# Recurrence of 64-token chunks on one core: the triangular inverse's products of odd chunks placed on the crossed corners of the TensorE array

## The reference

```
def step(s, inp):
    r_t, w_t, k_t, v_t, kk_t, b_t = inp
    sa = jnp.einsum('bhij,bhj->bhi', s, kk_t)
    s = s * w_t[:, :, None, :] - sa[..., None] * b_t[:, :, None, :] + v_t[..., None] * k_t[:, :, None, :]
    return s, jnp.einsum('bhij,bhj->bhi', s, r_t)
```

## Time and profile before

| | us |
|---|---|
| median of 3 runs | 3148.85 (3147.89 to 3151.09) |
| the profiled execution's own time | 3144.85 |
| its span, first to last instruction | 3143.1 |
| recurrence, twelve passes (2066 to 2577) | 511.0 |
| PE busy in them | 437.73 |
| DVE busy in them | 337.21 |
| ACT busy in them | 245.44 |
| POOL busy in them | 237.93 |

### The profile page before, as it was taken

How to read it: one execution, slowest core, us unless ns; L and a number is a source line. 1 busy time by engine, 2 the same in 40 slices (tenths; PEclk the granted TensorE clock), 3 DMA queues, 4 the chain that set the end, 5 groups by cost and what they waited for, 6 DMA issues and landing times. The chain is left out here.

```text
span 3143.1 us, 59081 instructions
## 1 busy us (share of the span) xinstructions
PE 2825.9 (90%) x25000; PEld 2232.2 (71%) x25000; DVE 1862.5 (59%) x2779; ACT 1153.1 (37%) x2127; POOL 1023.7 (33%) x582
## 2 busy tenths in 40 slices
PE   7999898999989998999999799978888887699987
PEld 5765576877867655777878587857777775479975
DVE  6888656885059786478840466466666654354062
ACT  4234434333242334343321422244454533242252
POOL 1422142444424221334443222244444430132202
PEclk9999899999999999999999899989999997899988
DMA  6321123433323211244332423210000003033111
GB/s 214 94 77 51 42 87 96 147 114 90 98 80 91 74 41 55 74 136 144 117 88 81 127 78 104 81 49 23 4 24 23 24 8 137 31 111 91 54 38 54
DMA packets 349911, 247.85 MB, mean 79 GB/s; under 512 B 10811, under 2 KB 322385, under 8 KB 349137
## 3 DMA queue, kind: packets, MB, share of 16 engines
q1 hardware_dynamic: 342384, 228.05, 24.0%
q10 hardware_dynamic: 7264, 16.03, 1.6%
HBM read 221.59 MB, written 16.52 MB: 76 GB/s over the span
## 5 line engine op out<-in xcount | busy, mean ns | idle before, releaser
L540 POOL TENSOR_TENSOR weights_lo<-weights_raw,weights_hi 128x1024 fp32r<-128x1024 f32 (+2 forms) x230 | 582.0, 2531 | 1111.3 <-ACT weights_hi L509 1111.3
L1181 PE MATMUL psum<-moving_hi,weights_hi 128*128 128x512 f32 x1472 | 601.7, 409 | 40.5 <-PEq L178 13.7
L1181 PE MATMUL psum<-moving_lo,weights_hi 128*128 128x512 f32 x1472 | 581.7, 395 | 0.0
L1181 PE MATMUL psum<-moving_hi,weights_lo 128*128 128x512 f32 x1472 | 581.2, 395 | 0.0
L1181 PEld LDWEIGHTS psum<-moving_hi,weights_hi 128*128 128x128 f32 x1472 | 281.0, 191 | 160.8 <-issue 67.8
L509 ACT ACTIVATE weights_hi<-weights_raw 128x1024 fp32r<-128x1024 f32 (+1 forms) x240 | 248.3, 1036 | 249.3 <-PE psum L1181 244.5
L1181 PEld LDWEIGHTS psum<-moving_hi,weights_lo 128*128 128x128 f32 x1472 | 281.0, 191 | 60.8
L1181 PEld LDWEIGHTS psum<-moving_lo,weights_hi 128*128 128x128 f32 x1472 | 282.2, 192 | 56.3 <-issue 3.8
L2585 POOL TENSOR_TENSOR second_off<-second_mats,second_masks 128x256 f32<-128x256 f32 x180 | 140.7, 786 | 157.4 <-PE psum L2061 156.7
L2641 PE MATMUL psum<-hn_hi,even_hi 128*128 128x256 f32 x480 | 166.4, 347 | 8.6 <-DVE hn_lo L1998 7.7
L2641 PE MATMUL psum<-hn_lo,even_hi 128*128 128x256 f32 x480 | 164.1, 342 | 0.0
(11 more groups left out here) (468 smaller groups left out, 6137.7 us busy)
## 6 DMA issues: line engine op xcount, KB each, us to landing
weights_raw<-in_w_up SPq DMA_DIRECT2D x88, 512.0 KB, 3.7
weights_raw<-in_w_in SPq DMA_DIRECT2D x80, 512.0 KB, 3.7
ada<-in_ada_w SPq DMA_DIRECT2D x9, 2048.0 KB, 9.4
odd_raw<-in_od_w_in SPq DMA_DIRECT2D x16, 1024.0 KB, 5.5
even_raw<-in_ev_w_in SPq DMA_DIRECT2D x30, 512.0 KB, 4.0
weights_raw<-in_w_down SPq DMA_DIRECT2D x32, 448.0 KB, 3.7
weights_raw<-in_w_o SPq DMA_DIRECT2D x16, 512.0 KB, 4.0
weights_raw<-in_w_down SPq DMA_DIRECT2D x16, 512.0 KB, 3.9
```

Of the source, the lines that this page charges most:

```text
L540: ops.tensor_tensor(self.ring.lo[i % n][:, a:b], self.ring.raw[:, t % self.ring.landing, a:b], self.ring.hi[i % n][:, a:b].bitcast(F32), A ...
L1181: return nc.tensor.matmul(to, (hi, lo)[which][:, at:at + P], moving(k)[part], start=start and k == 0 and i == 0, stop=stop and k == n_k - ...
```

## The change

Chunks at odd places of a group (c = 1 and 3) keep their W<sup>T</sup> on the other head's half of the partitions (`turn_odd`, one transposition of 64 partitions for each half). Their Y is computed crossed, so it lies on the other half as well, and their increment is crossed back. Even chunks use the first bank of a pair and odd ones the second: Y lies in banks 0 and 1, the increment in banks 2 and 3, in each round. So Y(n) now waits for the copy of Y(n-1), and the increment of n-1 for the addition of n-2. At a group's beginning the whole transposition stays and `turn_odd` follows behind its own semaphore; after a level, one transposition of the two even chunks (`straight`) and the two of `turn_odd` take the place of the whole one. In the steps, p of an odd chunk stays crossed, since its W<sup>T</sup> is: its beginning becomes straight, its end and the u product crossed. The copy of Y and the addition go over the two banks in one instruction each, as before.

```diff
...
         return halves_matmul(self.nc, self.p, self.buf.ntrk[:, slot_of(self.i, self.order[k]), 0:CH], self.v(k),
-                             start=True, stop=k == 0, crossed=True)
+                             start=True, stop=k == 0, crossed=not self.turned(k))
+
+    def turned(self, k):
+
+        return (self.order[k] - self.starts[k // 4]) % 2 == 1
...
                 pe.wait_ge(self.state_ready, k)
-                halves_matmul(nc, self.p, b.ar[:, self.i % 3, n, 0:CH], b.st[:, k % 2, :], start=False, stop=True).then_inc(self.p_ready, 1)
+                halves_matmul(nc, self.p, b.ar[:, self.i % 3, n, 0:CH], b.st[:, k % 2, :], start=False, stop=True,
+                              crossed=self.turned(k)).then_inc(self.p_ready, 1)
                 self.begin_y(k - 1)
...
             pe.wait_ge(self.p_taken, k + 1)
-            halves_matmul(nc, self.u, b.wb[:, slot, 0:CH], self.p_sb).then_inc(self.u_ready, 1)
+            halves_matmul(nc, self.u, b.wb[:, slot, 0:CH], self.p_sb, crossed=self.turned(k)).then_inc(self.u_ready, 1)
             if k + 1 < NCH and (k % 4 or not g):
...
             over = lambda name: mask(name).unsqueeze(1).to_broadcast([P, 4, mask(name).shape[1]])
-            bank = lambda b, n: psum[:, b * 512:b * 512 + 4 * n].rearrange("p (c n) -> p c n", n=n)
...
                 .rearrange("p b (c n) -> p b c n", n=width)
-            bank_y, bank_w = lambda n: bank(n % 2, CH), lambda n: bank(2 + n % 2, CH)
+            bank_y, bank_w = (pair_of_banks(n, CH)[:, :, 0:2, :] for n in range(2))
+            straight = lambda x, g, to: x[:, slots(g).start:slots(g).start + 4:2, to]
+            turned = lambda x, g, to, hf: x[64 * hf:64 * hf + 64, slots(g).start + 1:slots(g).start + 4:2, to]
+            by_bank = lambda x: x.rearrange("p (c b) n -> p b c n", b=2)
+            T, W = slice(0, CH), slice(CH, 2 * CH)
             names = "unit_ready taken_act taken_dve wt_scaled wt_begun w_begun masked y_ready y_taken w_ready w_added wt_turned "
...
                             if level == 0:
-                                pe.wait_ge(w_begun, g + 1)
+                                pe.wait_ge(w_begun, 2 * g + 2)
                             else:
                                 pe.wait_ge(w_added, n - 2)
-                            if n >= 2:
-                                pe.wait_ge(y_taken, n - 1)
+                            if n:
+                                pe.wait_ge(y_taken, n)
                             for c in range(4):
-                                last = halves_matmul(nc, bank_y(n)[:, c, :], off[:, n % 2, c, :], buf.wb[:, slots(g).start + c, CH:])
+                                last = halves_matmul(nc, bank_y[:, c % 2, c // 2, :], off[:, n % 2, c, :], buf.wb[:, slots(g).start + c, CH:],
+                                                     crossed=c % 2 == 1)
                             last.then_inc(y_ready, 1)
...
                             pe.wait_ge(y_taken, n)
-                            if n > 2:
-                                pe.wait_ge(w_added, n - 2)
+                            if n > 1:
+                                pe.wait_ge(w_added, n - 1)
                             if level:
...
                                 wt, y_ = buf.wb[:, s0 + c, 0:CH], y[:, own(g).start + c, :]
-                                last = halves_matmul(nc, bank_w(n)[:, c, :], *((wt, y_) if level < last_level else (y_, wt)))
+                                last = halves_matmul(nc, bank_w[:, c % 2, c // 2, :], *((wt, y_) if level < last_level else (y_, wt)),
+                                                     crossed=level < last_level and c % 2 == 1)
                             last.then_inc(w_ready, 1)
...
                             act.wait_ge(y_ready, n + 1)
-                            S.activation(y[:, own(g), :], bank_y(n), ACT.Identity).then_inc(y_taken, 1)
+                            S.activation(by_bank(y[:, own(g), :]), bank_y, ACT.Identity).then_inc(y_taken, 1)
                         steps(len(units) + 2 * n)
...
+                    def turn_odd(g):
+                        for hf in range(2):
+                            last = V.transpose(turned(buf.wb, g, T, hf), turned(buf.wb, g, W, 1 - hf))
+                        return last
+
                     def begin_w(g):
                         dve.wait_ge(wt_begun, g + 1)
-                        V.transpose(buf.wb[:, slots(g), CH:], buf.wb[:, slots(g), 0:CH]).then_inc(w_begun, 1)
+                        V.transpose(buf.wb[:, slots(g), W], buf.wb[:, slots(g), T]).then_inc(w_begun, 1)
+                        dve.wait_ge(w_begun, 2 * g + 1)
+                        turn_odd(g).then_inc(w_begun, 1)
...
                                 dve.wait_ge(w_added, n - 1)
-                                V.transpose(buf.wb[:, slots(g), 0:CH], buf.wb[:, slots(g), CH:]).then_inc(wt_turned, 1)
+                                V.transpose(straight(buf.wb, g, T), straight(buf.wb, g, W))
+                                turn_odd(g).then_inc(wt_turned, 1)
                         if n:
...
                             w_ = buf.wb[:, slots(g), CH:] if level < last_level else buf.wb[:, slots(g), 0:CH]
-                            V.tensor_tensor(w_, w_, bank_w(n), ALU.add).then_inc(w_added, 1)
+                            V.tensor_tensor(by_bank(w_), by_bank(w_), bank_w, ALU.add).then_inc(w_added, 1)
                         steps(len(units) + 2 * n + 1)
...
```

## The result

The changed kernel takes 3200.4 us (3196.4 to 3204.1) against 3148.4 of before: 1.0166 times its time, interval 1.0154 to 1.0178, 52 us slower. The forecast was 3146 with a range up to 3168. The rest of the program is unchanged; the difference lies in the recurrence and its bare steps.

What follows compares the result with a forecast made beforehand. Compute and its hand-overs, not DMA, bound the recurrence. Passes -4.8, -2, +1, -2.5, corners +2.2 and clock +3 sum to -3.1 us, taking the 3148.85 median to 3146; range 3124 to 3168, the forecast's own 3140 to 3153.

Steps and rivals of the forecast that it cites:

- Takes away: TensorE's products in the rounds: 27 of 30 per pass become half crossed, each 0.21 us shorter, 68 us in all.
- Adds: VectorE's transpositions: 0.66 us a turn, 0.31 more, 45 us; groups' beginnings 0.91 instead of 0.35, 20 us; together 65 us.
- Makes wait: One pair of banks: first products wait for ScalarE's copy (costed at nothing), second products for VectorE's addition (not at nothing).
- The sum by passes: Recurrence: five passes with few terms -4.8 us, five with many -2, first pass +1, last pass -2.5.
- The clock: TensorE sparser in the rounds: three or four more halved-clock stretches, 3 us; as a rival 12 us, 3155, chance 0.08.
- The corners of p and u: Odd chunks' products in the state's steps change corners: 1 us lost in the passes, 1.2 us in the end steps.
- Additions over two banks: VectorE's additions and ScalarE's copy over two banks: same elements, no added cost; 0.02 us each on 180 would be 4.
- Both signs: Forecast wrong to the slow side if transposition halves take 0.3 us apart, or the halved clock fills a quarter of the stage.
- VectorE becomes the bound: Rival, chance 0.20: second products wait for the addition just before, VectorE's operations stop TensorE too; about +19 us, 3168.

Runs made afterwards that it cites:

- single banks: The kernel before with one bank for each of the two products instead of two in turn, and the waits this needs; 3168.5 us, ratio 1.0069.
- whole turns: The changed kernel with one whole transposition per turn and at the groups' beginnings, so odd chunks get other numbers; 3152.7 us, ratio 1.0015.
- the kernel of turns alone: The kernel before with three-part turns, odd chunks on their own half, and two transpositions added at groups' beginnings; 3180.4 us, ratio 1.0106.

## Why the prediction was wrong

The differences of the runs, put one on the other: turns on their own half +33, single banks on top of them +14, crossed corners -13, the shift between halves in the turns +17; together 52 (51 by the rounded parts), which they must be, since each difference is taken from the kernel ahead of it. The parts depend on the order: with the banks first they are +22, crossed corners -17, turns +30, the shift +17. In either order the turns with their shift are 47 to 50 us, and single banks and crossed corners nearly cancel. The steps of the prediction, in its order:

- *Takes away* (0.21 us of TensorE in each of 324 products, 68 us): the product's size was right. What it is worth was not: 13 us with the longer turns beside it, 17 with whole turns. Where VectorE's round is the floor, a shorter product only waits longer.
- *Adds* (0.66 a turn, 65 us on VectorE): this is the step that failed first. Measured are 0.98 and 118 us (98 by busy time). The bounds held it (0.31 more was taken, 0.63 came, 0.70 was the upper one), but the value was taken from the nearest row by size, two copies of 128 columns, and those copies overlap (0.28 long, 0.21 apart) where these transpositions don't (0.31 long, 0.32 apart). The row of the same operation was the better neighbour: three whole ones would have been 1.05. The Trainium skill's page "VectorE: DVE Perf Modes", section on the TRN2 errata, would by its 58 cycles and one per column have had a half transposition at an estimated 0.19 us; measured are 0.31 for one alone and 0.32 from start to start. The same section of the Trainium skill says that this row comes out too low for a single operation, which the prediction passed over.
- *Makes wait* (the copy's wait at nothing, the addition's not priced by itself): single banks cost 22 us alone. The chain was put right in the text (0.05 of release, 0.26 of product, 0.27 until it is seen), but it was not read as a floor: with an addition it is 1.0 us a round, above the 0.87 that two banks allowed. Changing 0.87 to 1.08 in the first pass alone was too little; the floor stands in every dense round.
- *The sum by passes*: the first pass was to be 1 us longer and is 10 from start to start (36.7 to 46.8), at a clock of 0.65 on average; the last was to be 2.5 shorter and is 1.6 longer (33.2 to 34.8); the ten others were to lose 7 in all and gained 39 (3.5 each with few terms beside, 4.3 with many).
- *The clock* (3 us): the stretches at 1.2 GHz came, 116 us more and not the few forecast; that they cost the time was not borne out, since 65 us fewer of them changed nothing that could be told. How much they cost in the first pass stays open: there 22 us more of halved clock and 3.6 us more of time came together with the crossed corners.
- *The corners of p and u* (2.2 us): the bare steps are 1.0 us longer in the profile, within the bounds. What the corners cost in the passes was not measured apart.
- *Additions over two banks* (nothing): right. They took 421 ns in the mean against 405 before, but 420 in the kernel of turns alone, which has the banks of before.

Both signs that the prediction named for the slow side came: parts of a turn 0.32 apart, and the halved clock in 161 of 561 us, over a quarter. Of the rivals, "VectorE becomes the bound" named the place and the mechanism; its 3168 was worked out with the same 65 us and was too low. The Trainium skill's "TensorEngine Tiling (Array Packing)", section on the PSUM bottleneck, which was put beside that rival, agrees with the trace: TensorE's second products gave up time and got 43 us of waits instead of 1.3, most of them for the copy and the addition, which empty the banks.

## What to carry to other kernels

Before a product is halved, work out the floor of its round with the buffers that remain: the chain from the reader's end through release, product and its way back, and each engine's own work; the larger of the two is the limit of the gain, and here both rose while the product fell. Price an instruction that is cut into smaller ones from a row of the same operation, and take the upper bound where none shows it. Where a profile shows the halved clock on the path, as in the kernel before, a few products that nobody reads in TensorE's wait gave 20 us; in the changed kernel, where VectorE sets the pace of the dense rounds, they gave nothing that could be told.

## What the hardware showed

- Of two transpositions of 128 columns, the second overlapped the first (0.23 us from start to start at 0.31 long) where both read and wrote from the same first partition on. It started only at the end of the one ahead where it lay on the other half of the partitions, or read from one half and wrote to the other (0.32, or 0.27 behind one of 0.26). Three of them took 0.85 and 0.98 us. The addition behind them started 0.34 after the last one's start in both, 0.03 after its end, where before it started 0.08 ahead of the whole transposition's end. All these rows fit one reading: an instruction waits for the end of the one ahead when its input or its output begins on another half than that one's. No run tests this by itself.
- Straight and crossed products of one round overlap in two banks: 16 records in 0.25 us instead of 0.47, as the unit in the earlier trace rows had shown.
- With TensorE's records doubled in the rounds, 65 us of idle time came in the passes for which the trace names no cause, 57 of them not behind an addition; most ended 1.2 to 1.6 us after a 16 KB packet of the "instruction" queue had landed.
